# HGRN's level products between the blocks of the MLA attention, its final factors under the mLSTM

## What is computed

```python
for l in range(DEPTH):                                  # 2 layers
    x = x + 0.5 * post1(swiglu(pre1(x)))
    u = pre2(x) @ w_in                                  # columns split among the three mixers
    mix = concat(mla(u), mlstm(u), hgrn2(u)) @ w_out
    x = x + post2(mix)
    x = x + 0.5 * post3(swiglu(pre3(x)))
```

```python
b = jnp.cumsum(lfc, axis=1)
diff = b[:, :, None] - b[:, None]
dec = jnp.exp(jnp.where(causal[None, :, :, None, None], diff, -jnp.inf))
a = jnp.sum(qc[:, :, None] * kc[:, None] * dec, axis=-1)
o = jnp.einsum('btsh,bshv->bthv', a, ic) + jnp.einsum('bthd,bhdv->bthv', qc * jnp.exp(b), s)
s_new = jnp.exp(b_last)[..., None] * s + jnp.einsum('bshd,bshv->bhdv', kc * jnp.exp(b_last[:, None] - b), ic)
```

## Time and profile before

| | us |
|---|---|
| median of 3 runs | 3158.11 |
| the profiled execution, its time | 3161.45 |
| its span, first to last instruction | 3159.6 |
| PE busy | 2866.4 (91%) |
| DVE busy | 1301.6 (41%) |
| ACT busy | 894.0 (28%) |
| POOL busy | 367.0 (12%) |
| the three mixers with their preparation, first layer | 664 to 1031 |
| the same, second layer | 2217 to 2586 |

### The profile page before, as it was taken

The page is one execution under the profiler, slowest core; times in us unless marked ns, Lnnn a source line. Parts: engine busy times, 40 slices in busy tenths (PEclk is TensorE's granted clock), DMA queues, the critical chain, the costliest instruction groups (busy, mean ns, idle before and its releaser), DMA issues.

```text
span 3159.6 us, 44981 instructions
## 1 busy us (share of the span) xinstructions
PE 2866.4 (91%) x18622; PEld 2697.2 (85%) x18622; DVE 1301.6 (41%) x1732; ACT 894.0 (28%) x1112; POOL 367.0 (12%) x322
## 2 busy tenths in 40 slices
PE   6999998988766899999989999989786778999997
PEld 6999998965455799999989999989454668999997
DVE  3332335434277453333353333354334665333234
ACT  4221224224322332212342212241344123321222
POOL 0100110011113101001101000110111211110110
PEclk9999999989857999999999999999887579999998
DMA  3222223310102212222322222232001101223212
GB/s 113 70 72 77 78 59 94 88 33 1 28 13 18 73 54 73 74 80 57 89 56 74 70 80 70 77 86 76 19 9 27 22 22 54 80 59 88 80 55 72
DMA packets 367467, 191.00 MB, mean 60 GB/s; under 512 B 36677, under 2 KB 363128, under 8 KB 367358
## 3 DMA queue, kind: packets, MB, share of 16 engines
q1 hardware_dynamic: 363550, 179.09, 21.2%
q0 software_dynamic: 3808, 10.38, 1.1%
HBM read 183.51 MB, written 5.93 MB: 60 GB/s over the span
## 4 chain that ended last, share of the span: by engine, by line
PE 84%; DVE 7%; ACT 4%; issue 2%; DMA 1%; SPq 1%; POOL 0%; DVEq 0%; ACTq 0%; POOLq 0%
PE ps L546 24%; PE ps L548 24%; PE ps L547 24%; PE ps L717 1%; DVE at L1842 1%; PE ps L739 1%; DMA out_dram<-css 1%; DVE qkc L1743 1%; ACT wh L1101 1%; PE ps L757 1%; PE ps L748 1%; PE ps L789 1%; PE ps L725 1%; PE ps L790 1%; ACT r L1101 1%
## 5 line engine op out<-in xcount | busy, mean ns | idle before, releaser
L546 PE MATMUL ps<-xh,wh 128*128 128x320 f32 x3456 | 1080.5, 313 | 67.4 <-DVE xl L1493 44.4
L547 PE MATMUL ps<-xl,wh 128*128 128x320 f32 x3456 | 1077.7, 312 | 0.0
L548 PE MATMUL ps<-xh,wl 128*128 128x320 f32 x3456 | 1077.4, 312 | 0.0
L546 PEld LDWEIGHTS ps<-xh,wh 128*128 128x128 f32 x3456 | 657.1, 190 | 72.2 <-issue 59.1
L547 PEld LDWEIGHTS ps<-xl,wh 128*128 128x128 f32 x3456 | 657.2, 190 | 0.0
L548 PEld LDWEIGHTS ps<-xh,wl 128*128 128x128 f32 x3456 | 656.7, 190 | 0.0
L1448 DVE TENSOR_TENSOR wl<-raw,wh 128x2048 fp32r<-128x2048 f32 x180 | 420.3, 2335 | 438.7 <-ACT wh L1101 438.7
L1101 ACT ACTIVATE wh<-raw 128x2048 fp32r<-128x2048 f32 x181 | 344.7, 1904 | 481.5 <-PE ps L548 466.6
L548 PE MATMUL ps<-hh,wl 128*128 128x320 f32 x1408 | 435.7, 309 | 0.0
L547 PE MATMUL ps<-hl,wh 128*128 128x320 f32 x1408 | 435.7, 309 | 0.0
L546 PE MATMUL ps<-hh,wh 128*128 128x320 f32 x1408 | 435.7, 309 | 0.0
(11 more groups left out here) (338 smaller groups left out, 2906.7 us busy)
## 6 DMA issues: line engine op xcount, KB each, us to landing
raw<-in_w_ffn_in_dram SPq DMA_DIRECT2D x178, 512.0 KB
raw<-in_w_ffn_out_dram SPq DMA_DIRECT2D x64, 384.0 KB
raw<-in_w_ffn_out_dram SPq DMA_DIRECT2D x64, 320.0 KB
raw<-in_w_in_dram SPq DMA_DIRECT2D x38, 512.0 KB
raw<-in_w_out_dram SPq DMA_DIRECT2D x16, 512.0 KB
out_dram<-xio SPq DMA_DIRECT2D x5, 512.0 KB, 2.7
xio<-in_x_prompt_dram SPq DMA_DIRECT2D x1, 2048.0 KB
y<-in_cache_ckv_dram POOLq DMA_DIRECT2D x8, 256.0 KB, 3.2
```

Of the source, the lines that this page charges most:

```text
L546: pe.matmul(out, wh, xh, start=first, stop=False)
L547: pe.matmul(out, wh, xl, start=False, stop=False)
L548: return pe.matmul(out, wl, xh, start=False, stop=last)
```

## The change

- DD0, QK0, DD1, LVL, AT and QK1 move into the memory of WH and WL, which become one tile W with both parts of a slot side by side.
- The 37 level steps move from `hgrn` into `mla`. `LEVEL_EARLY` and `LEVEL_LATE` say after which block each stands: in the blocks i == 2 and i == 3 of the first seven heads, two to a block (an early one after the scores, a late one after the values), and two in each of the last four blocks, one behind them. They all use banks 0 and 1, so each PE step waits for the copy of the step before (`lv_sb(m - 1)`). `head_prep` waits for the last copy of the head (`lv_sb`).
- `distances` stand on POOL behind the product of each head's rotation, `decays` on ACT after blocks 3, 7, 12, 16 and 20, `scaled` on DVE after blocks 7, 10, 15, 22 and 26. The first two of each stand in the preparation of `mla`. POOL zeroes AT there. The masks are loaded as bytes, with no cast.
- KDF and QE are made in `mlstm`: distances on POOL behind VMSK, exponentials on ACT and products on DVE at t == 2, where level 0 stood.
- The split of the first unit of `wout` moves from the end of `proj` to the end of `mlstm` on ACT and into `hgrn` at t == 2 on DVE. On SP `mixers` stands ahead of the load of the third unit of `wout`.
- In `hgrn` PE waits for `hg_in` (the states SS) before the last tile. OWN2 and its load go. Several small tiles change their place.

```diff
+LEVEL_STEPS = [(n, t) for n in range(NLEV) for t in range(PT_ if n < 3 else TILES)]
+LEVEL_EARLY, LEVEL_LATE = {}, {}
+for _h in range(H - 1):
+    LEVEL_EARLY.update({PT_ * _h + 2: 4 * _h, PT_ * _h + 3: 4 * _h + 2})
+    LEVEL_LATE.update({PT_ * _h + 2: 4 * _h + 1, PT_ * _h + 3: 4 * _h + 3})
+for _i in range(PT_):
+    LEVEL_EARLY[PT_ * (H - 1) + _i] = 4 * (H - 1) + 2 * _i
+    LEVEL_LATE[PT_ * (H - 1) + _i] = 4 * (H - 1) + 2 * _i + 1
+SCALED_AFTER = {7: 2, 10: 3, 15: 4, 22: 5, 26: 6}
+DECAYS_AFTER = {3: 2, 7: 3, 12: 4, 16: 5, 20: 6}
...
@@ tensor, mla
+        def level_step(l, m):
+
+            n, t = LEVEL_STEPS[m]
+            if t == 0:
+                if n < NLEV - 1:
+                    pe.wait_ge(*hq_sb.nth(l, n))
+                else:
+                    pe.wait_ge(*kk_sb.nth(l, 0))
+            if m:
+                pe.wait_ge(*lv_sb.nth(l, m - 1))
...
+                mm = pe.matmul(PS[:, h % 2, h // 2 * P:h // 2 * P + P], k_, q_, start=True, stop=True)
+            mm.then_inc(lv_ps.sem, 1)
...
+            if h >= 2:
+                pe.wait_ge(*lv_sb.nth(l, LEVEL_LATE[PT_ * (h - 2) + 3]))
...
                     attend_scores(l, n + 2)
+                if n in LEVEL_EARLY:
+                    level_step(l, LEVEL_EARLY[n])
                 if n + 1 < NT:
                     attend_transpose(l, n + 1)
...
                 attend_values(l, n)
+                if n in LEVEL_LATE:
+                    level_step(l, LEVEL_LATE[n])
+            level_step(l, NLV - 1)
             pair_output(l, H // 2 - 1)
+            pe.wait_ge(*lv_sb.nth(l, NLV - 1))
...
@@ vector, mla
                 maximum(n)
+                if n - 2 in LEVEL_EARLY:
+                    level(LEVEL_EARLY[n - 2])
                 if n >= 3:
                     normalise(n - 3)
-            for n in range(NT - 3, NT):
-                normalise(n)
+                if n - 2 in LEVEL_LATE:
+                    level(LEVEL_LATE[n - 2])
+                if n in SCALED_AFTER:
+                    scaled(l, SCALED_AFTER[n])
+            for n in range(NT - 2, NT):
+                level(LEVEL_EARLY[n])
+                normalise(n - 1)
+                level(LEVEL_LATE[n])
+            normalise(NT - 1)
+            level(NLV - 1)
...
@@ scalar, mlstm
                 if t == 2:
-                    decays(l, 0)
+                    act.wait_ge(*kd_sb.nth(l, 0))
+                    run(KDF[:, :, :], KDF[:, :, :], ACT.Exp)
+                    run(EBL[:, :, 0:PT_], BC[:, :, ENDS_P], ACT.Exp)
+                    run(EBL[:, :, PT_:12], BC[:, :, ENDS_S], ACT.Exp)
+                    run(QE[:, :, :], BC[:, :, :], ACT.Exp).then_inc(qe_sb.sem, 1)
...
@@ vector, mlstm and hgrn
                 if t == 2:
-                    scaled(l, 0)
+                    dve.wait_ge(*qe_sb.nth(l, 0))
+                    V.tensor_tensor(KDF[:, :, :], KDF[:, :, :], KK[:, :, :], ALU.mult).then_inc(kd_sb.sem, 1)
+                    V.tensor_tensor(QE[:, :, :], QE[:, :, :], HQ[:, :, :], ALU.mult).then_inc(qe_sb.sem, 1)
...
+                if t == 2:
+                    split_lo(l, WOUT, 0, 0)
...
@@ gpsimd, mla
+                if 1 <= h < NLEV - 2:
+                    pool.wait_ge(*qc_sb.nth(l, h))
+                    held(pool)
+                    distances(l, h + 1)
+                    pool.wait_ge(*hd_sb.nth(l, h + 1))
```

More of the change, by code:

```diff
@@ L266, in encoder @@
     QM2 = tile(s_w, "qm2", [P, 2, NSEQ, P])
+    tile(s_w, "gap_states", [P, 512 + 260 + 2080])
     IM = tile(s_w, "im", [P, NSEQ, MH * DK])
[L268 to L277, removed]
+    tile(s_w, "gap_decays", [P, KD * T + (KD // 2) * T - 2 * 2048 - 2852])
     SS = tile(s_w, "ss", [P, 2, NSEQ, P])
@@ L468, in bring @@
                 sp.dma_start(dst, src).then_inc(s, 16)
+            sp.wait_ge(unit_done, unit(l, PROJ, 0, 9) + 3)
+            bring(level_in, LVL[:, :, :], A["c_level"])
             sp.wait_ge(*mla_done.nth(l, 0))
@@ L1220, in mla @@
             run(GB[:, :, :], GB[:, :, :], ACT.Exp, scale=-0.5).then_inc(mla_r.sem, 1)
+            for n in range(2):
+                decays(l, n)
             act.wait_ge(*tok_ps.nth(l, 0))
@@ L1277, in mla @@
                     probabilities(n + 2)
+                if n in DECAYS_AFTER:
+                    decays(l, DECAYS_AFTER[n])
             pair_output(H // 2 - 1)
@@ L1371, in hgrn @@
         def hgrn(l):
-            for n in range(1, NLEV - 1):
-                decays(l, n)
-            act.wait_ge(*kd_sb.nth(l, 0))
-            run(KDF[:, :, :], KDF[:, :, :], ACT.Exp)
-            run(EBL[:, :, 0:PT_], BC[:, :, ENDS_P], ACT.Exp)
-            run(EBL[:, :, PT_:12], BC[:, :, ENDS_S], ACT.Exp)
-            run(QE[:, :, :], BC[:, :, :], ACT.Exp).then_inc(qe_sb.sem, 1)
             for t in range(TILES):
@@ L1645, in normalise, with level @@
                                 ALU.mult).then_inc(on_sb.sem, 1)
+            def level(m):
+                n, t = LEVEL_STEPS[m]
+                if m == 0:
+                    dve.wait_ge(level_in, (l + 1) * 16)
+                    dve.wait_ge(*at_zero.nth(l, 0))
+                else:
+                    dve.wait_ge(*lv_sb.nth(l, m - 1))
+                dve.wait_ge(*lv_ps.nth(l, m))
+                held(dve)
+                V.copy_predicated(AT[:, t, :, :, :],
+                                  LVL[:, n, :].unsqueeze(1).unsqueeze(1).broadcast_to([P, 2, 2, P]),
+                                  PS[:, 0:2, 0:256].rearrange("p e (g t) -> p e g t", t=P)).then_inc(lv_sb.sem, 1)
+            scaled(l, 0)
+            scaled(l, 1)
             head(0)
@@ L2025, in mla @@
                 cache(b)
+            pool.wait_ge(unit_done, unit(l, PROJ, 0, 9) + 3)
+            held(pool)
+            distances(l, 0)
+            distances(l, 1)
             pool.wait_ge(*kpe_ready.nth(l, 0))
```

152 lines of the change are left out of this document (59 added, 93 removed).

## The result

The changed kernel takes 3166.41 us (median of 11 runs, 3161.96 to 3175.74). The kernel before, run beside it, takes 3157.83 (11 runs, 3151.59 to 3161.14). The ratio is 1.003, 95% interval 1.002 to 1.0041: slower by 0.3%, where 3128 was forecast. The profiled execution took 3164.75 us with a span of 3162.9, 3.3 us above that of before.

The account below looks back on a forecast made before the run. PE bounds the attention but not the level part, 57.1 us a layer and all that can be won. Per layer -57.1 + 23.8 + 5.7 + 2 + 8.0 + 0.4 + 2 = -15.2; 3158.1 - 30 = 3128 us, range 3091 to 3150.

Parts of the forecast that it names:

- level part and mLSTM: Level products leave their own stretch before the recurrence, -57.1 us a layer; DVE's two products in the mLSTM add 0.4.
- steps in seven heads and the last one: 37 level steps in the attention: 23.8 us a layer for seven heads plus 8.0 for the last.
- POOL beside the rotation: In five heads of the attention POOL's distances slow DVE's rotation end: 2 us a layer, bounds 0 and 4.4.
- `scaled` between the blocks: DVE's `scaled` products in the attention delay copies or the rotation: 2 x 1.3 + 3 x 1.05 = 5.7 us a layer.
- recurrence without the states: More of the recurrence's first tiles run at the low clock: 2 us a layer, bounds 0 to 5.
- wait for the states: PE's new wait for the states SS before the recurrence's last tile: about zero, bounds 0 and 4 us.
- The hand schedule of one head: Attention head laid out by hand with the steps in it: 3.4 us more a head, 1 us of it waiting at `head_prep`.
- The rival in which the steps vanish: Attention steps mostly vanish into slack, only 21.6 us of PE time a layer remaining: 3091 us, chance 0.18.
- that in which each pays its round trip: All 37 attention steps pay 1.71 us, 63.3 a layer, on the single pair of banks: 3190 us, chance 0.08.
- the clock: PE's waits drop the attention's granted clock to 0.71, 82 us of PE work becoming 113: 3190 us, chance 0.05.
- The rival "not whole": Recurrence waits 4 us a layer for SS before its last tile, port at its upper bound: 3141 us, chance 0.14.

Follow-up runs that it names:

- feed moved: Changed kernel with DVE's `scaled` and ACT's decays behind other blocks and POOL's distances waiting until the rotation has ended: 3118.38 us, ratio 0.9883.
- `scaled` moved: Changed kernel with only `scaled` and decays behind other blocks, POOL's distances left as they were: 3124.69 us, ratio 0.9905.
- states first: Changed kernel with the four loads of the states SS ahead of the eight mLSTM state stores on SP: 3145.94 us, ratio 0.9973.
- the order of `head_prep` moved as well: Changed kernel with states first, feed moved, and the bank-2 product of `head_prep` ahead of its wait for the last level copy: 3088.8 us, ratio 0.9791.
- The filler at the head's end: Changed kernel with three unread PE products at the end of each head, none before the rotation: 3181.95 us, ratio 1.0089.

## Why the prediction was wrong

Step by step, for the first layer (forecast, then measured):

| term | forecast | measured | from |
|---|---|---|---|
| start | 0 | +0.15 | milestones |
| level part and mLSTM | -57.1 + 0.4 | -58.6 | milestones |
| streams | 0 | -1.4 | milestones |
| steps in seven heads and the last one | +31.8 | +32.3 | feed moved |
| POOL beside the rotation | +2 | +2.2 | `scaled` moved |
| `scaled` between the blocks | +5.7 | +21.3 (14.8 in layer 2) | changed kernel less `scaled` moved |
| recurrence without the states | +2 | +0.1 | states first |
| wait for the states | 0 | +8.3 | states first |

The row of the steps holds what `scaled` costs at the better blocks as well.

**Right: the steps.** The hand schedule of one head, with one pair of banks and a round trip of 1.71 us, gave 3.4 us a head and 8.0 for the last. With the feed moved the second to the seventh head are 3.6 to 3.7 us longer than before. The last head, 15.2 by my sum, runs from 838.28 to 853.47, 15.2 us:

```profile
838.28 0.91 PE L776 MATMUL ps<-kt,qt 96*128 96x384 f32 x2
...
853.47 0.66 PE L803 MATMUL ps<-ident,y 128*128 128x128 f32 x4
```

The rival in which the steps vanish (3091) is out, and so is that in which each pays its round trip (63 us a layer): they cost 32.3. With the order of `head_prep` moved as well they cost 131.8 - 107.0 = 24.8, not far from the 21.6 of PE time which the first rival kept.

**Failed: the price of `scaled`.** I gave it 2 x 1.3 + 3 x 1.05, with products of 0.69 to 0.83 us. Three things were wrong. First, the price of the product: I had the row of 1.70 us beside POOL and used it for the rotation alone. But the blocks i == 2 are just where POOL makes its own part of the rotation (L2086) and the distances, so the first product took 1.66 and 1.69 us after blocks 22 and 26, and both were slow after block 10. The Trainium skill, "GPSIMD Engine Reference", section Specifications, which the prediction used for the rotation, names every VectorE instruction with two SBUF inputs, so `scaled` falls under it as well; here the trace agrees, with 1.66 and 1.87 us for 0.82, and 2.11 for 1.25 on POOL's side. Second, I took 0.2 us of slack and one delay for each place, while at block 10 the whole pair of 3.5 us stood ahead of the rotation, and the scores of the next head behind it. Third, and largest, I priced a delay at its length. These are the first layer's attention in the changed kernel and with `scaled` moved:

```profile
690.67:853.47 162.80, 137.71 (x740) 88.69 (x740) 83.28 (x190) 52.84 (x136) 27.89 (x18) 0.86 0.00 1
```
```profile
689.08:830.61 141.53, 121.48 (x741) 78.36 (x741) 79.76 (x190) 52.40 (x136) 27.53 (x18) 0.98 0.00 1
```

Of the 21.3 us only 25.1 - 20.1 = 5.0 are PE standing longer (L776 waits 7.6 us for L1654, and 2.5 with `scaled` moved). The other 16.2 are PE busy for longer with the same products, at the lower clock. In the second layer the same division is 5.9 and 8.9.

**Failed: the clock got 0.05.** That rival had the mechanism: PE stands for DVE, and the granted clock falls. It was priced at 0.71 over the whole attention, 3190 us, and argued away with "it kept 0.98 with gaps of 1.2 us". That argument holds only for gaps as they were. In the changed kernel PEclk is 0.87, by which the loss is smaller than I priced the rival, and it came with the `scaled` places, not with the steps: with the feed moved, the steps' waits are all there and PEclk is 0.98. I had treated the delay and the clock as two cases to choose between, when moving the delay took both away. The Trainium skill, "TensorE: Matmul & The Clock Gate", section "HAM oscillation", says that waits between bursts throttle PE again; by the changed kernel's rows the trace agrees. The filler at the head's end, with less waiting and a lower clock, shows that it isn't the whole story.

**Failed: the states "about zero".** Need at 17.3 us plus 2 was near (16.7). Arrival was not: I took 21.4 less 2 to 4 for the masks, and it was 22.2. My 2 to 4 us for the masks had no row behind them, and without the masks the states came no earlier. In the changed kernel the eight stores take 5.51 us on the queue and the loads behind them 12.43 to issue; ahead of the stores they take 2.79. The second layer of before had 2.75 for them behind the same stores, but the first layer, which I hadn't read beside it, had 8.46. The last of them landed 20.8 and 21.1 us after the level part began in the two layers. Why it was some 1 us later still without the masks stays open.

```profile
954.10 8.46 SPq L468 DMA_DIRECT2D ss<-in_state_hgrn_dram  x4
```

And the price of a wait of 5.6 us was 8.3, since the last tile behind it ran at the low clock: once more the clock was added to a wait. The rival "not whole" (3141) had this wait at 4 us, which was also my upper bound; neither had the clock behind it.

**The sum, redone.** -15.2, + 0.5 (steps), + 0.2 (port), + 15.6 (`scaled`), - 3.3 (level part, mLSTM and streams), + 6.4 (recurrence and states, 8.4 for 2), + 0.15 (start) = +4.35; measured +4.3. The two failed terms make 22 us of the miss in the first layer and 14 in the second (9.1 for `scaled`, 5.0 for recurrence and states). With `scaled` at better blocks the same forecast would have been too high: feed moved, which still waits for the states, takes 3118.

What stays open: why the first layer's attention took 162.8 us and the second's 156.3 in one execution of the same instructions (the clock stood longer at 0.50 in the first; states first has 156.2 in both), and which pattern of PE's idle time lets it fall.

## What to carry to other kernels

When work is put into an engine's slack, lay out by hand who waits for that engine at that very point, and which other engine runs beside it there; a place one or two blocks earlier was worth 15 to 21 us a layer here. Don't count on filling the gaps either: unread products gave 14 us back at two places and cost 19 at one. Price a delay of PE twice, once as a wait and once with the clock at half speed for the work behind it. And in a DMA queue put the loads that something waits for ahead of the stores that nothing does.

## What the runs showed of the hardware

- DVE's products with two SBUF operands took 1.66 to 1.87 us beside POOL's two-operand work instead of 0.82, also where only a product of 32 partitions stood beside them (L2086, after blocks 22 and 26). L1652, with one operand in PSUM, stayed at 0.82. POOL's distances took 1.62 and 2.11 us there, and 1.25 each is the time of one alone; L2086 itself stayed at 1.53.
- PEclk fell to 0.50 within a gap of 2.73 us and stayed there for some 9 us after it, though PE was fully busy. It fell also behind three gaps of 0.30, 0.53 and 0.97 us close together, with no long one; with 0.29 for the last of them it didn't.
- Unread products on PE made a kernel 14 us faster (ratio 0.9985 against 1.003), at two places of a head together. At the one ahead of the rotation alone they made it 10 us faster (0.9998), at the head's end alone 19 us slower (1.0089), with less idle time of PE and a lower clock.
- Four loads of 128 KB took 12.43 us to issue and 11.6 to land behind eight stores on the same queue, and 2.79 and 3.2 ahead of them. In the kernel before, behind the same stores, they took 8.46 us to issue in one layer and 2.75 in the other.
